# A chain of transformer blocks on one core: three raw-weight slots and five split-weight slots in place of four and four

## The reference

```python
h = hybrid_mixer(x, ...)            # x @ w_in, windowed + dense attention, gating, w_branch, w_mix_out
x = layer_norm(ALPHA * x + h, ln1_g[l], ln1_b[l])
h = memory_cross_attention(x, mem, x_wq[l], x_wkv[l], x_wo[l])
x = layer_norm(ALPHA * x + h, ln2_g[l], ln2_b[l])
h = conv_ffn(x, f_w_up[l], f_conv_k[l], f_conv_b[l], f_w_down[l])
x = layer_norm(ALPHA * x + h, ln3_g[l], ln3_b[l])

def conv_ffn(x, w_up, conv_k, conv_b, w_down):
    h = x @ w_up                                    # 1024 x 5632
    h = sum(hp[:, j:j + S] * conv_k[j] for j in range(CONV_W)) + conv_b
    a, b = jnp.split(h, 2, axis=-1)
    return (gelu(a) * b) @ w_down                   # 2816 x 1024
```

## Time and profile before

| | |
|---|---|
| median of 3 runs | 3880.23 us (3877.24 to 3884.49) |
| the profiled execution | 3883.91 us, its span 3882.1 us |
| TensorE busy | 3602.2 us (93%) |
| GpSimd busy | 2070.2 us (53%) |
| VectorE busy | 1597.0 us (41%) |
| ScalarE busy | 1014.5 us (26%) |
| granted clock of TensorE, mean | 0.959 |
| DMA | 345.19 MB, 89 GB/s on the mean |

### The profile page before, as it was taken

One profiled execution on the slowest core, in us unless ns is written; L12 is line 12 of the kernel. 1 busy time (PEld: TensorE's weight loads), 2 busy tenths in 40 slices (PEclk: granted clock), 3 DMA queues, 4 the chain that ended last, 5 costly groups with the idle time before them and its releaser, 6 DMA issues.

```text
span 3882.1 us, 44893 instructions
## 1 busy us (share of the span) xinstructions
PE 3602.2 (93%) x17537; PEld 2791.5 (72%) x17537; DVE 1597.0 (41%) x2437; ACT 1014.5 (26%) x1955; POOL 2070.2 (53%) x2126
## 2 busy tenths in 40 slices
PE   7999997999898999879998899998899989989998
PEld 5677775888676777758886666776688767667886
DVE  3465434655325653356553554233422143233222
ACT  1344224212123441232112453333211023212111
POOL 4444572667543445726675453443566634346664
PEclk9999999999999999989998999999899989999998
DMA  4122321655221213325652222221333222122332
GB/s 133 55 66 60 87 85 52 202 178 171 80 66 49 66 50 94 91 61 173 189 157 72 55 68 60 71 55 57 86 94 98 87 66 64 45 76 82 97 91 67
DMA packets 578697, 345.19 MB, mean 89 GB/s; under 512 B 15935, under 2 KB 561976, under 8 KB 578488
## 3 DMA queue, kind: packets, MB, share of 16 engines
q1 hardware_dynamic: 574541, 337.34, 29.8%
q10 hardware_dynamic: 3947, 4.99, 0.4%
HBM read 340.14 MB, written 2.14 MB: 88 GB/s over the span
## 4 chain that ended last, share of the span: by engine, by line
PE 85%; DVE 7%; ACT 5%; issue 1%; POOL 0%; DMA 0%; SPq 0%; ACTq 0%; DVEq 0%; POOLq 0%
PE gemm L220 23%; PE gemm L223 22%; PE gemm L226 22%; PE outs L299 6%; PE scores L299 6%; PE gemm L255 1%; PE scores L1417 1%; PE gemm L256 1%; PE gemm L257 1%; ACT tiles L633 1%; DMA w_raw<-in_w_in 0%; DVE x_t L1084 0%; DVE tiles L1081 0%; DVE scales L702 0%; DVE work L1406 0%
## 5 line engine op out<-in xcount | busy, mean ns | idle before, releaser
L199 POOL CAST w_high<-w_raw 128x512 fp32r<-128x512 f32 (+1 forms) x1061 | 692.9, 653 | 1695.7 <-PE gemm L226 1289.5
L201 POOL TENSOR_TENSOR w_low<-w_raw,w_high 128x512 fp32r<-128x512 f32 (+1 forms) x1061 | 1388.2, 1308 | 84.9
L220 PE MATMUL gemm<-x_high,w_high 128*128 128x512 f32 x2584 | 724.1, 403 | 25.0 <-POOL w_high L199 6.5
L223 PE MATMUL gemm<-x_low,w_high 128*128 128x512 f32 x2584 | 701.2, 394 | 0.0
L226 PE MATMUL gemm<-x_high,w_low 128*128 128x512 f32 x2584 | 695.1, 391 | 0.0
L220 PEld LDWEIGHTS gemm<-x_high,w_high 128*128 128x128 f32 x2584 | 480.2, 191 | 137.2 <-issue 17.4
L223 PEld LDWEIGHTS gemm<-x_low,w_high 128*128 128x128 f32 x2584 | 491.4, 190 | 106.7
L226 PEld LDWEIGHTS gemm<-x_high,w_low 128*128 128x128 f32 x2584 | 488.2, 189 | 104.2
L220 PE MATMUL gemm<-split_tiles,w_high 128*128 128x512 f32 (+1 forms) x1456 | 399.1, 395 | 21.2 <-DVE split_tiles L538 9.5
L223 PE MATMUL gemm<-split_tiles,w_high 128*128 128x512 f32 (+1 forms) x1456 | 388.6, 388 | 0.0
L226 PE MATMUL gemm<-split_tiles,w_low 128*128 128x512 f32 (+1 forms) x1456 | 386.2, 386 | 0.0
(11 more groups left out here) (342 smaller groups left out, 3613.3 us busy)
## 6 DMA issues: line engine op xcount, KB each, us to landing
w_raw<-in_mlp_w SPq DMA_DIRECT2D x112, 512.0 KB, 4.0
w_raw<-in_mod_w SPq DMA_DIRECT2D x96, 512.0 KB, 3.9
w_raw<-in_w_in SPq DMA_DIRECT2D x88, 512.0 KB, 3.8
w_raw<-in_f_w_up SPq DMA_DIRECT2D x88, 512.0 KB, 5.0
w_raw<-in_e_w_in SPq DMA_DIRECT2D x48, 512.0 KB, 4.0
w_raw<-in_f_w_down SPq DMA_DIRECT2D x32, 512.0 KB, 4.2
w_raw<-in_o_w_in SPq DMA_DIRECT2D x30, 512.0 KB, 3.9
w_raw<-in_w_branch SPq DMA_DIRECT2D x48, 256.0 KB, 2.7
```

The source lines that it names most:

```text
L199: me.pool.tensor_copy(WH[:, h, 0:n], W32[:, s, c0:c0 + n]).then_inc(sem["w_rounded"], 1)
L201: me.pool.tensor_tensor(WL[:, h, 0:n], W32[:, s, c0:c0 + n], WH[:, h, 0:n].bitcast(F32), ALU.subtract).then_inc(sem["w_split"], 1)
L220: me.pe.matmul(o, WH[:, h, (k - k0) * cols:(k - k0 + 1) * cols], src(k)[0], start=begin and k == 0, stop=False)
L223: me.pe.matmul(o, WH[:, h, (k - k0) * cols:(k - k0 + 1) * cols], src(k)[1], start=False, stop=False)
```

## The change

One raw slot is given up and a fifth split slot is added. Both constants size the buffers, the semaphores of landing (one for each raw slot) and the modulus by which `fetch` and `split_piece` choose slots and what they wait for; nothing else uses them. A raw slot is 4 KB of each partition, a split slot 2 KB for `w_high` and 2 KB for `w_low`, so the sum stays the same.

```diff
@@ -36,8 +36,8 @@
 ODD_IN = 3840
 NEG = -1.0e30
 WMAX = 8
-WRING = 4
-HRING = 4
+WRING = 3
+HRING = 5
 HWIDE = 512
 TT = 24
 RT = 24
```

## The result

The changed kernel takes 3912.93 us (median of 4 runs, 3911.84 to 3915.61); the kernel before took 3878.73 on the same chip (4 runs, 3876.85 to 3884.49; the 3880.23 of the table above is the median of the first three). The ratio is 1.0085, with a 95% interval of 1.0071 to 1.0099: 34 us slower, where 24 were forecast. The profiled execution of the changed kernel took 3912.59 us (span 3910.8), 28.7 more in the span than the one before.

The account below looks back on a forecast made before the run. TensorE's split gemm bounds the kernel, and rings matter only where weights come late; +25.0 us in conv_ffn and -1.2 at x_wq give +23.8, forecasting 3904.0 us. The forecast's own case is 3898 to 3916, the full range 3882 to 3938.

Parts of the forecast that it names:

- What bounds it: Split gemm on TensorE bounds the kernel; ring sizes matter only where TensorE waits for a weight, or would with other rings.
- The slot arithmetic: conv_ffn, unit i's weights Wi, modulation load Mi: with three raw slots Wi waits for M(i-2)'s read, one unit (5.5 us) later.
- The cost of one load: conv_ffn: 4.73 us from the end of VectorE's modulation read to TensorE's start, through issue, 3.9 us transfer and cast.
- The cascade: conv_ffn: shortfalls at even units outside `down`, median about 0.8 us, accumulate to 12.4 us in layer 0, 12.6 in layer 1.
- rival B: conv_ffn, heavier: Mi waits for the split of W(i-1), next W lands in 5.0 us, casts contended; 3926 us; chance 0.22.
- The pairs of x_wq: Pair of x_wq units in each layer: the fifth split slot gains up to 2.3 us in all, half kept, -1.2.
- The sum: Whole kernel: +25.0 in conv_ffn and -1.2 at x_wq give net +23.8 us, 3904.0 as median.
- A: Rival, conv_ffn: no change, the modulation reads come early enough and the shortfall vanishes; 3879 us; chance 0.16.
- C: Rival, conv_ffn: a load alone in its queue lands in 3.5 us or less, cascade +17; 3896 us; chance 0.10.
- D: Rival, faster: x_wq pairs gain the whole 2.3 us, TensorE's clock isn't lowered, conv_ffn loses nothing; 3874.5 us; chance 0.05.

Follow-up runs that it names:

- order34: Against the kernel before: three raw and four split slots, with the next unit's weights fetched ahead of the modulation load in conv_ffn; 3883.03 us, ratio 1.0004.
- order35: Against the changed kernel (three raw, five split slots): the next unit's weights fetched ahead of the modulation load in up and first down; 3880.49 us.
- late2_35: Against the changed kernel: VectorE issues `gated` after the next modulation read, and the first of each eight reads ahead of `mod_out`'s copy; 3887.5 us.
- again44: A copy of the kernel before, four raw and four split slots, nothing changed, run once more; 3885.02 us.
- r3s4: Against the kernel before: three raw slots, the four split slots kept, so the raw slot is given up alone; 3911.87 us, ratio 1.0071.
- shift35: Against the changed kernel: second layer's eight parameter-load steps stand behind units 22 to 29 instead of 4 to 11, their uses 17 units later; 3911.32 us.
- dense35: Against the changed kernel: the small e_D loads in the second layer's conv_ffn read eight adjacent values instead of every second one; 3916.78 us.

## Why the prediction was right, and where its terms were off

**What bounds it.** Right. The ring matters where a weight is late, and that is conv_ffn. Outside conv_ffn and x_wq three raw slots cost nothing that can be measured: order34 keeps three and is at 1.0004.

**The slot arithmetic (Wi takes the slot of M(i-2)).** Right. order35 changes the place of a load in the queue and with it whose slot it takes, and the loss is gone. late2_35 changes nothing but when VectorE gives the slot back, and all but some 2 us a layer are gone as well. The two act on the two ends of the one wait.

**The cost of one load, 4.73 us.** Right. The stalled units of layer 0 start 4.6 to 5.15 us behind the end of their read, median 4.8, except W6 (5.47). The latency fit of the Trainium skill that the prediction weighs (DMA: Bandwidth & Descriptors, two cost components) is given there for loads that GpSimd issues; these are issued by SyncE, and W8's took 3.83 us. The landing of f_w_up fell from 5.0 to 4.4, not to 3.9.

**The cascade, +12.4 and +12.6.** The mechanism was right and the size too small, which the +12.9 of layer 0 hides: 1.6 us of the loss are made up by W2, which ran at the low clock in the kernel before and at the full one in the changed one. The stalls cost 14.5. That W10 was due 1.60 us late behind W2 and came 1.62 late is luck: against again44, with W2 at the same clock, it came 3.2 late. Two terms are missing in my sum. It took its starts from a kernel whose slow W2 gave the next loads 1.6 us more time, and it began at W6; with a fast W2 already W3 waited 0.27 us, and W6 and W8 more than was due. And some 0.1 us per stall: the first four matmuls behind a stall take 1.01 us, those in the flow 0.91, and there were 14 stalls. Forecast were about 17 places a layer. None was in `down`, as forecast.

In layer 1 the term was mis-sized more: +16.4 for +12.6, or 18.0 with W2 at the same clock. Beside the two terms above, two causes show in the trace. W9 and W10 landed late beside the parameter loads (W10 6.00 us behind its read). And rival B's mechanism occurred, in single places. At W20, where VectorE's table work had delayed the read and TensorE idled 3.12 us, the late split of W20 held the next modulation load, and W22 stood behind that one. Waits of SyncE from 1865 to 1872, then GpSimd and TensorE:

```profile
SPq L185 <- POOL w_low L201: 6.0, 1, 6.0
```

```profile
1869.16 1.29 POOL L201 TENSOR_TENSOR w_low<-w_raw,w_high 128x512 fp32r<-128x512 f32 x1
...
1878.14 1.16 PE L220 MATMUL gemm<-x_high,w_high 128*128 128x512 f32 x4 [0.51 <-POOL w_high L199]
```

The split of W20 ended at 1870.45, M21 went out at 1870.48 and W22 at 1870.86, 6.5 us ahead of its cast. My cascade had only the read of M(i-2) in it, and no chain from a late W to the next M. It gave B as a whole case; it is a term that follows each large stall.

**The pairs of x_wq, -1.2.** Wrong in sign: +2.8. The first half of the step held: the pair starts on x_low, and the idle ahead of it fell from 3.39 to 2.12 us. But GpSimd's casts, which had waited for a split slot, now ran while VectorE made the x_low. Changed kernel, VectorE, GpSimd and TensorE:

```profile
571.81 1.79 DVE L685 SCALAR_TENSOR_TENSOR x_low<-work,layer_params,x_high 128x512 fp32r<-128x512 f32 x1
574.19 1.80 DVE L685 SCALAR_TENSOR_TENSOR x_low<-work,layer_params,x_high 128x512 fp32r<-128x512 f32 x1
...
577.90 1.81 DVE L685 SCALAR_TENSOR_TENSOR x_low<-work,layer_params,x_high 128x512 fp32r<-128x512 f32 x1
...
577.87 1.29 POOL L201 TENSOR_TENSOR w_low<-w_raw,w_high 128x512 fp32r<-128x512 f32 x1
...
579.76 0.50 PE L255 MATMUL gemm<-x_high,w_high 128*128 128x512 f32 x1 [0.68 <-DVE x_low L685]
```

The third and fourth are as slow in the kernel before. The sixth and seventh took 1.81 us each, where they took 0.98 and 1.12, and TensorE's idle behind x_low L685 grew from 4.9 us in 2 places to 13.7 in 11. An L685 that GpSimd leaves alone takes 0.74. The figure fits the rule of the Trainium skill (SBUF — State Buffer, the rules on the shared port pair) that a VectorE operation with two SBUF inputs and GpSimd's reads block each other for a whole instruction; I had weighed it in conv_ffn and forgot it here. r3s4, with four split slots, has 0.0, and so it is throughout: the seven profiles with five split slots have +1.2 to +1.5 in each layer, the six with four -0.1 to +0.1.

**The sum.** Forecast +25.0 - 1.2 = +23.8, with +18 to +36 as its own range, which holds the result; measured in the profiles +29.3 + 2.8 = +32.1 and -3.4 elsewhere, 28.7. That the result is so near has some luck in it: the stalls cost 32.5 us for the 25.0 forecast and x_wq 4.0 more than forecast, and W2's clock (-3.2) and the other stages (-3.4) took most of that back. The medians differ by 34.2; the 5.5 us between the two are what single executions of one program differ by.

**The rivals.** A (no change) fell: L538 still takes 1.68 us ahead of M6's read at W8, and the stalls are there. C (a short transfer) fell with the landing of 3.83 us at W8. D fell with the sign of x_wq and the loss in conv_ffn. B happened at single units.

## What to carry to other kernels

A ring of slots that is shared by two kinds of loads in one in-order queue has to be read as a table: which load takes whose slot, and which engine gives that one back, and when. Going from four to three slots changed not the room but the partner, from weights to a read that an unrelated queue of work delays; an issue order that gives the urgent loads the slots of users that are done earlier recovered all of it without memory. And a stage time from one profiled execution has to be compared at the same granted clock before its difference is put down to an edit: here one slow matmul group was worth 1.6 us a layer. Work that is made to start earlier on one engine has to be looked at for what it now runs beside.

## What the hardware showed that was not expected

- A 2 KB load in 4-byte pieces (e_D, every second value, 64 partitions; the second of two, the first took 0.66) took 2.93 us to issue in shift35 and 1.99 in the changed kernel; read side by side in dense35 each took 0.59. Around it, from 1900.1 to 1903.6 us, the transfers of the core moved at most 58 GB/s and at times none, and a 512 KB load ahead of it in the queue took 11.4 us to its cast; the median landing of such loads (f_w_down) is 4.1 in the changed kernel.
- A weight load with small parameter loads issued right behind it came late: 8.9 us from the issue of W11 to its cast in dense35, 7.2 in the changed kernel, 5.7 in the kernel before. No run took these small loads away, so that they are the cause isn't shown.
- The same idle of 1.82 us ahead of the same matmul was followed by a clock of 0.58 in one execution of a program and of full speed in another: 1.6 us a time. In the mixer of layer 0 the slow stretches lay elsewhere too: from 172 to 184 us the granted clock was 1.00 in the kernel before and 0.71 to 0.72 in again44, and the stage ended 5.2 us later.
